# Angles, peaks and tables moved between a pair's maximum and its scale, and one-column sums set between long products

## The chip, the cores and the metric

One core of one Trainium2 chip runs the whole kernel in one launch. The metric is the device time of that core in microseconds (us), median of several runs. The engines are called PE (TensorE, matrix products), DVE (VectorE), ACT (ScalarE), POOL (GpSimd) and SP (SyncE, which here only issues DMAs). PSUM is where PE writes.

## The reference, cut to what matters

```python
# layer 0: x -> x + concat(pool mixer, short conv mixer, each gated by silu) @ w_out_ab
# layer 1, for 1024 tokens, 1024 channels, 16 heads:
h = rms_norm(x, norm_c)
c_q, c_kv, k_rope, z = split(h @ w_in_c, [768, 1024, 1056])
q  = rms_norm(c_q, q_lat_norm) @ w_uq      # needs the mean square of c_q over 768 channels, per token
kv = rms_norm(c_kv, kv_lat_norm) @ w_ukv   # and of c_kv over 256 channels
cos, sin = cos(positions * inv_freq), sin(positions * inv_freq)
q, k = rope_tail(rms_norm(q, q_head_norm), cos, sin), rope_tail(rms_norm(k, k_head_norm), cos, sin)
x = x + (causal_attention(q, k, v) * silu(z)) @ w_out_c
```

Everything is float32. The change lies in the first half of layer 1: the input projection `h @ w_in_c`, the tables of cosine and sine, and the mean squares of `c_q` and `c_kv`.

## The kernel before, in words

Channels lie on the 128 partitions, the 1024 tokens along the free dimension. Each engine has one program, in a fixed order, written out by hand as a function (`sync`, `scalar`, `vector`, `gpsimd`, `tensor`); semaphores join them. An engine does nothing behind a wait until the wait is over. Numbers are split into a high and a low part, and every product is made of three matmuls (`three_passes`, lines 111 to 113): high by high, high by low, low by high.

Layer 1's input projection has two kinds of output tiles. The four plain gate tiles `Z0` to `Z0+3` (the last is `ROPE0-1`) and the tile `ROPE0` of the rotary key are products with float32 parts, 48 matmuls a tile, 32 for `ROPE0`, each 128x512. The other twelve tiles are made two at a time, as pairs 8 to 13 (`PAIRED` is 8, `GATE_PAIRS` is 12, `ALL_PAIRS` is 14): pairs 8 to 11 give the latents `c_q` and `c_kv`, pairs 12 and 13 the last four gate tiles. A pair is made Strassen-like from seven products (`pair_product(p, i)`, i from 0 to 6) of float16 parts; each is 12 matmuls of 128x512, in four chunks `c` of three.

For a pair p+1 to be ready, this chain runs while PE works on pair p:

- DVE takes the largest weight of the raw tiles (`pair_peak`, line 1071, out `w_row`); PE spreads it over partitions with one one-column float32 product against `ones` (`row_sum`, line 1562) after product 2 of pair p, and waits there if the maximum is late;
- DVE turns it into a scale (`pair_scale`, lines 1080 to 1082), after which ACT writes the seven high parts (`pair_forms`, line 720) and DVE the seven low parts (`pair_low`, line 1088);
- between them DVE makes three quarters of pair p's output from PSUM (`quarter`, line 1101) as products 3, 4 and 5 of it end, and ACT makes snapshots of products 0, 1 and 2 (`snapshot`, line 727). Product i of 2, 3, 4 waits for snapshot i-2, and product 6 waits for the second quarter. POOL makes the sums of raw weights that four of the forms need (`left_sums`), and adds squares of the latents (`square_sums`, line 634).

Other work of DVE hangs in this loop at the end of an iteration: `angles(0)` and `angles(1)` (the rotary angles, brought into the range of the sine), `peaks` (the largest weights of `w_ukv`), `tables` (14 table and gain instructions, lines 1145 to 1158, from the sine that ACT makes at line 873), `rope_and_roots` (line 1164 on, which begins with the mean squares of the latents and ends with the semaphore `roped`). The mean squares come from 16 one-column products of PE with the squares as weights (line 1599), all in a row after product 5 of pair 12. In the same way `token_sums` (line 1617) makes 8 in a row inside tile `Z0`.

In the last pair DVE writes the low parts of six latents (`lat_low`, line 1209) and of the first weights of the next stage (line 1318). The next stage's first product waits for `roped`, for all eight `lat_low` and for all eight low parts of those weights. The gates of pair 12 are multiplied by the roots by POOL (line 649), those of pair 13 by DVE (`late_gate`, line 1260).

Of the kernel before, what the change touches and what calls it, by code (L numbers as in the profile page):

```python
# [20 lines left out]
ALU = mybir.AluOpType  # L21
AX_X, AX_XY = mybir.AxisListType.X, mybir.AxisListType.XY

P = 128
# [162 lines left out]
def front(nc, x_t, gamma, w_in, pool_w, pool_scale, conv_w, w_out, x1_t, gamma1, w_lat, positions, q_lat_g, kv_lat_g,  # L187
# [408 lines left out]
    def gpsimd(pool):  # L596
# [47 lines left out]
        for m in range(2):  # L644
            dest_m = pair_dest(GATE_PAIRS, m)
            pool.wait_ge(c_done, 3 * (GATE_PAIRS + 1))
            pool.wait_ge(c21_done, GATE_PAIRS + 1)
            pool.wait_ge(roped, 1)
            nc.gpsimd.tensor_tensor(dest_m, dest_m, rstd_all[:], ALU.mult).then_inc(gate_scaled, 1)

    def scalar(act):
# [210 lines left out]
        def later_paired():  # L862
            for p in range(PAIRED, ALL_PAIRS):
                last_pair = p + 1 == ALL_PAIRS
                late_square = PAIRED + 2 <= p < GATE_PAIRS
                if PAIRED < p <= GATE_PAIRS:
                    latent_squares(p - 1, range(1 if late_square else 2))
                snapshot(p, 0)
                if p == PAIRED:
                    plain_silu(PLAIN_GATES - 1)  # L870
                if p == PAIRED + 1:
                    act.wait_ge(reduced, 2)
                    nc.scalar.activation(trig[:], red[:], ACT.Sin).then_inc(trig_done, 1)
                if p == GATE_PAIRS - 1:
                    latent_high(1)
                if p == GATE_PAIRS:
                    latent_high(3)
                if last_pair:
                    latent_high(0)
                snapshot(p, 1)  # L880
                if p == GATE_PAIRS - 1:
                    latent_high(2)
                if p == GATE_PAIRS:
                    latent_high(4)
                if last_pair:
                    for m in (KQ, KQ + 1):
                        latent_high(m)
                if late_square:
                    latent_squares(p - 1, [1])
                snapshot(p, 2)  # L890
                if last_pair:
                    latent_high(KQ - 1)
                if not last_pair:
                    pair_forms(p + 1, range(FORMS))
                else:
                    first_weights()
                last_quarter(p)
            act.wait_ge(gate_scaled, 2)
            for m in range(2):
                gate_silu(PLAIN_GATES + m)  # L900
            act.wait_ge(last_scaled, 2)
            for m in range(2):
                gate_silu(PLAIN_GATES + 2 + m)
# [39 lines left out]
    def vector(dve):  # L943
# [312 lines left out]
        def late_gate(m):  # L1256
            dest_m = pair_dest(GATE_PAIRS + 1, m)
            dve.wait_ge(c_done, 3 * ALL_PAIRS)
            dve.wait_ge(c21_done, ALL_PAIRS)
            nc.vector.tensor_tensor(dest_m, dest_m, rstd_all[:], ALU.mult).then_inc(last_scaled, 1)  # L1260
# [6 lines left out]
        def later_paired():  # L1267
            for p in range(PAIRED, ALL_PAIRS):
# [3 lines left out]
                if p == PAIRED:  # L1272
                    angles(0)
                if p == GATE_PAIRS - 1:
                    top()
# [4 lines left out]
                else:  # L1280
                    for j in range(2, LAT - 1):
                        lat_low(j)
# [20 lines left out]
                if p == PAIRED:  # L1303
                    angles(1)
                if p == PAIRED + 1:
                    peaks()
                if p == PAIRED + 2:
                    tables()
# [4 lines left out]
            for m in range(2):  # L1313
                late_gate(m)
# [121 lines left out]
        right_sums(0)  # L1436
        roots(2, ms1, rstd1, tmp1, sums[:, 0])
        right_sums(1)
        rights(0)
# [19 lines left out]
    def tensor(pe):  # L1459
# [26 lines left out]
        def tile(n):  # L1486
            pe.wait_ge(lo_done, n - RING + len(STEPS) + 1)
            slot_free(n)
            if n == Z0:
                for k in range(NK):  # L1490
                    pe.wait_ge(x1_done, k + 1)
                    for c in range(2):
                        last = product(n, k, c, k == 0, k == NK - 1)
                    if k == CHUNKS:
# [3 lines left out]
                    if k == NK - 2:  # L1498
                        pe.wait_ge(x1_added, OUT_TILES - 1)
                        token_sums()  # L1500
            else:
                for c in range(2):
                    for k in range(NK):
                        if n == OUT0 - 1 and c == 0 and k == CHUNKS:
                            row_sum(0)
                        if n == ROPE0 - 1 and c == 1 and k == CHUNKS:
# [6 lines left out]
        def first_out_tiles():  # L1513

            for part in (range(NK - 2), range(NK - 2, NK)):
                for n in (OUT0, OUT0 + 1):
# [7 lines left out]
                    if part.stop == NK:  # L1524
                        last.then_inc(proj_ready, 1)

        def pair_product(p, i):
# [17 lines left out]
            for c in range(CHUNKS):  # L1545
                if p == 0 and i in (2, 4, 6):
                    pe.wait_ge(act_low, FIRST_FORMS + (i // 2 - 1) * CHUNKS + c + 1)
                if p == PAIRED:
# [3 lines left out]
                                    right(p, i, 0, c), right(p, i, 1, c), fresh and c == 0, c == CHUNKS - 1, not fresh)  # L1552
            last.then_inc(pair_ready, 1)

# [18 lines left out]
        def later_paired():  # L1573
            for p in range(PAIRED, ALL_PAIRS):
                for i in range(FORMS):
# [17 lines left out]
                    if p == GATE_PAIRS and i == 5:  # L1593
                        pe.wait_ge(topped, 2)
                        pe.wait_ge(lat_summed, LAT - 2)
                        for part in range(2):
                            for t in range(NT):
                                col = part * NT + t
                                last = nc.tensor.matmul(small_ps[:, col:col + 1], sq[:, part, t * P:(t + 1) * P],
                                                        ones[:, 0:1], start=True, stop=True)  # L1600
                        last.then_inc(small_ready, 1)
# [12 lines left out]
        def token_sums():  # L1614

            for t in range(NT):
                last = nc.tensor.matmul(pooled[:, t:t + 1], sums[:, 0, t * P:(t + 1) * P], ones[:, 0:1],
                                        start=True, stop=True)
            last.then_inc(summed, 1)
# [982 lines left out]
```

## Time and profile before

| | |
|---|---|
| median of 3 runs | 995.08 us (995.02 to 995.61) |
| the profiled execution | 995.0 us, span 993.2 us |
| mean granted TensorE clock | 0.988 of 2.4 GHz |
| PE busy | 968.5 us, 98% of the span |
| DVE busy | 796.8 us, 80% |
| ACT busy | 563.2 us, 57% |
| POOL busy | 319.1 us, 32% |

Busy means that the engine had an instruction in work; a share near 100% of one engine says that it bounds the time, though not that each of its instructions ran at full speed. The granted clock says at which speed PE was let run: 1.00 is 2.4 GHz, 0.50 is 1.2 GHz. The span runs from the first to the last instruction; 1.8 us of the execution's time lie around it.

### The profile page before, as it was taken

The numbers are of one execution on the slowest core, as the hardware profiler recorded it, in microseconds if no ns is written. First come the engines' busy times: TensorE is split into PE (matmuls) and PEld (weight loads), VectorE is DVE, ScalarE is ACT, GpSimd is POOL, SyncE is SP. The second block draws the span as 40 slices with busy tenths as digits, with TensorE's granted clock in tenths as the row PEclk, the third lists the DMA queues.
The fourth block names the chain that finished last, engine by engine and source line by source line (L and its number), as shares of the span: only waits on it lengthen the run. The fifth ranks groups of instructions, "written<-read, shape, count | busy, mean of one in ns | idle before, by whom it ended". The sixth has DMA issues, their size and how long they took to land.

```text
span 993.2 us, 16008 instructions
## 1 busy us (share of the span) xinstructions
PE 968.5 (98%) x5858; PEld 709.3 (71%) x5858; DVE 796.8 (80%) x1363; ACT 563.2 (57%) x1049; POOL 319.1 (32%) x381
## 2 busy tenths in 40 slices
PE   9999999999999998989799999999999999999998
PEld 8788444444788887534356999997777888887887
DVE  5798899998765599878687799998999999996311
ACT  7443554335243372535437667867999999997000
POOL 0002342240000002236133477876864335551000
PEclk9999999999999999989889999999999999999999
DMA  9310421111154430413022164567587656430322
GB/s 296 61 50 12 111 80 43 45 41 43 64 170 146 129 86 19 153 44 82 1 69 81 37 213 137 204 196 187 112 212 155 160 127 115 108 108 1 116 85 75
DMA packets 165341, 103.65 MB, mean 104 GB/s; under 512 B 75272, under 2 KB 149520, under 8 KB 165008
## 3 DMA queue, kind: packets, MB, share of 16 engines
q1 hardware_dynamic: 159216, 102.25, 36.7%
q10 hardware_dynamic: 6048, 0.39, 0.5%
q8 instruction: 47, 0.77, 0.3%
q14 instruction: 30, 0.25, 0.1%
HBM read 56.48 MB, written 29.36 MB: 86 GB/s over the span
## 4 chain that ended last, share of the span: by engine, by line
PE 79%; DVE 16%; issue 3%; ACT 2%; DVEq 0%; POOL 0%; ACTq 0%; POOLq 0%
PE banks L111 22%; PE banks L113 22%; PE banks L112 22%; PE banks L2405 6%; PE banks L2423 3%; PE banks L2424 1%; DVE front_w_row L1071 1%; DVE lat_lo L1209 1%; DVE heads_probs_big L2213 1%; DVE front_lt L1229 1%; PE banks L1635 1%; PE banks L2432 1%; ACT heads_probs_big L2086 1%; DVE heads_pt_lo L2221 1%; DVE front_l L1229 1%
## 5 line engine op out<-in xcount | busy, mean ns | idle before, releaser
L2221 DVE TENSOR_TENSOR heads_pt_lo<-banks,heads_pt_hi 128x512 f16<-128x512 f32 (+2 forms) x192 | 102.0, 554 | 11.3 <-ACT heads_pt_hi L2095 6.9
L2095 ACT ACTIVATE heads_pt_hi<-banks 128x512 f16<-128x512 f32 (+2 forms) x192 | 88.4, 485 | 4.9 <-PE banks L2405 4.7
L2423 PE MATMUL banks<-heads_v,heads_pt_hi 128*128 128x128 f16 x576 | 74.6, 220 | 0.0
L2405 PE MATMUL banks<-ident,heads_probs_big 128*128 128x128 f32 x416 | 69.1, 279 | 1.4 <-ACT heads_probs_big L2086 1.3
L2424 PE MATMUL banks<-heads_v,heads_pt_lo 128*128 128x64 f16 x576 | 69.5, 193 | 0.0
L2213 DVE CUSTOM_DVE_ANT_0 heads_probs_big<-banks,heads_mask,score_scale 128x1024 f32<-128x1024 f32 (+1 forms) x64 | 68.5, 1071 | 0.9
L2086 ACT ACTIVATE heads_probs_big<-heads_probs_big,heads_neg_max 128x1024 f32<-128x1024 f32 (+1 forms) x64 | 63.4, 991 | 5.3 <-DVE heads_neg_max L2213 3.3
L111 PE MATMUL banks<-front_act_hi,front_w_hi 128*128 128x512 f32 x160 | 64.4, 403 | 0.0
L111 PE MATMUL banks<-heads_k_t,heads_q_t 96*128 96x512 f16 (+2 forms) x192 | 62.9, 327 | 0.9 <-DVE heads_neg_max L2213 0.9
L112 PE MATMUL banks<-front_act_lo,front_w_hi 128*128 128x512 f32 x160 | 62.9, 393 | 0.0
L113 PE MATMUL banks<-front_act_hi,front_w_lo 128*128 128x512 f32 x160 | 62.8, 393 | 0.0
L112 PE MATMUL banks<-heads_k_t,heads_q_t 96*128 96x512 f16 (+2 forms) x192 | 62.3, 324 | 0.0
L113 PE MATMUL banks<-heads_k_t,heads_q_t 96*128 96x512 f16 (+2 forms) x192 | 61.5, 325 | 0.0
L1747 DVE TENSOR_TENSOR out_res<-banks,out_res 128x512 f32<-128x512 f32 x16 | 10.9, 690 | 59.5 <-PE banks L113 59.5
L2423 PEld LDWEIGHTS banks<-heads_v,heads_pt_hi 128*128 128x128 f16 x576 | 54.1, 99 | 1.1 <-DVE heads_pt_lo L2221 0.3
L2338 POOL TENSOR_TENSOR heads_o_sum<-heads_o_raw 128x256 f32<-128x256 f32 x32 | 23.3, 728 | 94.0 <-ACT heads_o_raw L2102 93.6
L2424 PEld LDWEIGHTS banks<-heads_v,heads_pt_lo 128*128 128x128 f16 x576 | 51.3, 98 | 2.2
L2405 PEld LDWEIGHTS banks<-ident,heads_probs_big 128*128 128x128 f32 x416 | 46.7, 141 | 7.7 <-DVE heads_pt_lo L2221 3.3
L111 PE MATMUL banks<-out_gate_hi,out_w_hi 128*128 128x512 f32 x128 | 50.4, 394 | 0.4 <-DVE w_out_lo L1728 0.2
L111 PE MATMUL banks<-front_y_hi,front_w_hi 128*128 128x512 f32 x128 | 50.0, 391 | 0.0
L113 PE MATMUL banks<-out_gate_hi,w_out_lo 128*128 128x512 f32 x128 | 49.9, 390 | 0.0
L112 PE MATMUL banks<-gate_lo,out_w_hi 128*128 128x512 f32 x128 | 49.8, 389 | 0.0
(435 smaller groups left out, 3027.6 us busy)
## 6 DMA issues: line engine op xcount, KB each, us to landing
qk_scratch<-heads_y SPq DMA_DIRECT2D x22, 512.0 KB, 3.6
front_x<-in_x_t SPq DMA_DIRECT2D x16, 512.0 KB, 5.1
front_raw<-in_w_in_ab SPq DMA_DIRECT2D x14, 512.0 KB, 5.1
qk_scratch<-heads_last_y SPq DMA_DIRECT2D x10, 512.0 KB, 4.1
front_w<-in_w_out_ab SPq DMA_DIRECT2D x8, 512.0 KB, 3.7
x_scratch<-front_x SPq DMA_DIRECT2D x8, 512.0 KB, 4.0
v_scratch<-heads_v SPq DMA_DIRECT2D x32, 128.0 KB, 3.0
heads_v_st<-v_scratch SPq DMA_DIRECT2D x8, 512.0 KB, 5.3
```

The costliest lines, as they stand in the source:

```text
L111: nc.tensor.matmul(out, w_hi, a_hi, start=first, stop=False, skip_group_check=resumed)
L112: nc.tensor.matmul(out, w_hi, a_lo, start=False, stop=False, skip_group_check=resumed)
L113: return nc.tensor.matmul(out, w_lo, a_hi, start=False, stop=last, skip_group_check=resumed)
L1229: nc.vector.scalar_tensor_tensor(right_split(c, part, 1), right_source(c, part), later_scale[:, 0:1], right_split(c, part, 0), ALU.mult, A ...
L2086: nc.scalar.activation(row, row, ACT.Exp, bias=neg_max[:, h % 2, i:i + 1], scale=-1.0, accum_out=total[:, h % 2, i:i + 1]).then_inc(exp_do ...
L2095: nc.scalar.activation(pt_hi[:, q % PIECES, :width], t_ps[:, banks[("piece", n, k)] % 3, :width], ACT.Copy).then_inc(pt_high, 1)
L2213: nc.vector.tensor_tensor_reduce(probs(n, 0, width), scores(i, 0, width), mask[:, S - width:], score_scale[:], 3e38, ALU.add, ALU.min, neg ...
L2221: nc.vector.tensor_tensor(pt_lo[:, q % PIECES, :width], t_ps[:, banks[("piece", n, k)] % 3, :width], pt_hi[:, q % PIECES, :width], ALU.sub ...
L2338: nc.gpsimd.tensor_tensor(o_sum[:, g % 2], raw[:, :, :VH], raw[:, :, VH:], ALU.add).then_inc(o_summed, 1)
L2405: last = nc.tensor.transpose(t_ps[:, b, r * P:(r + 1) * P], probs(n, j * P, (j + 1) * P), ident[:])
L2423: nc.tensor.matmul(out, pt_hi[:, q % PIECES, blk], v2[e][:, j, :], start=(j == 0), stop=False)
L2424: last = nc.tensor.matmul(out[:, :VH], pt_lo[:, q % PIECES, blk], v2[e][:, j, :VH], start=False, stop=(j == i))
```

## The change

Four things change, and no instruction's size:

1. On DVE, `angles(1)`, `peaks` and `tables` leave the end of iterations 8, 9 and 10 and stand in iterations 9, 10 and 11 behind `pair_peak` of the next pair and ahead of its `pair_scale`. `angles(0)` stands there already. ACT's sine (line 873) moves from behind snapshot 0 to behind snapshot 2 of pair 9.
2. PE's `row_sum(8)` moves from the middle of the second half of tile `ROPE0-1` into the middle of the first half of `ROPE0`.
3. The 16 one-column sums of the latents are set two by two behind the first, second and third chunk of products 3, 4 and 5 of pair 12 (eight places), and the 8 of `token_sums` two by two behind the last four groups of tile `Z0`. On DVE `right_sums(1)` and two low parts of `rights(0)` now stand ahead of `roots(2)`, which waits for those sums.
4. The multiplication of pair 12's two gate tiles goes from POOL to DVE, one each behind the first two `lat_low` of the last iteration.

```diff
@@ gpsimd
-        for m in range(2):
-            dest_m = pair_dest(GATE_PAIRS, m)
-            pool.wait_ge(c_done, 3 * (GATE_PAIRS + 1))
-            pool.wait_ge(c21_done, GATE_PAIRS + 1)
-            pool.wait_ge(roped, 1)
-            nc.gpsimd.tensor_tensor(dest_m, dest_m, rstd_all[:], ALU.mult).then_inc(gate_scaled, 1)
@@ scalar, later_paired
                 snapshot(p, 0)
-                if p == PAIRED + 1:
-                    act.wait_ge(reduced, 2)
-                    nc.scalar.activation(trig[:], red[:], ACT.Sin).then_inc(trig_done, 1)
...
                 snapshot(p, 2)
+                if p == PAIRED + 1:
+                    act.wait_ge(reduced, 2)
+                    nc.scalar.activation(trig[:], red[:], ACT.Sin).then_inc(trig_done, 1)
@@ vector, later_paired
                     pair_peak(p + 1)
                 if p == PAIRED:
                     angles(0)
+                if p == PAIRED + 1:
+                    angles(1)
+                if p == PAIRED + 2:
+                    peaks()
                 if p == GATE_PAIRS - 1:
+                    tables()
                     top()
...
                     pair_scale(p + 1)
                 else:
-                    for j in range(2, LAT - 1):
+                    for m in range(2):
+                        lat_low(2 + m)
+                        late_gate(GATE_PAIRS, m)
+                    for j in range(4, LAT - 1):
                         lat_low(j)
...
-                if p == PAIRED:
-                    angles(1)
-                if p == PAIRED + 1:
-                    peaks()
-                if p == PAIRED + 2:
-                    tables()
@@ vector
         right_sums(0)
+        right_sums(1)
+        rights(0, range(2))
         roots(2, ms1, rstd1, tmp1, sums[:, 0])
-        right_sums(1)
-        rights(0)
+        rights(0, range(2, SIX))
@@ tensor, tile
                         last = product(n, k, c, k == 0, k == NK - 1)
+                        if k >= NK - 2:
+                            if k == NK - 2 and c == 0:
+                                pe.wait_ge(x1_added, OUT_TILES - 1)
+                            turn = 2 * (k - NK + 2) + c
+                            token_sums(range(2 * turn, 2 * turn + 2))
...
-                    if k == NK - 2:
-                        pe.wait_ge(x1_added, OUT_TILES - 1)
-                        token_sums()
...
-                        if n == ROPE0 - 1 and c == 1 and k == CHUNKS:
+                        if n == ROPE0 and c == 0 and k == CHUNKS:
                             row_sum(PAIRED)
@@ tensor, pair_product
+                if p == GATE_PAIRS and i in LATENT_TURNS and c < CHUNKS - 1:
+                    for n in range(2):
+                        latent_sum(6 * LATENT_TURNS.index(i) + 2 * c + n)
...
+        def latent_sum(col):
+            if col == 0:
+                pe.wait_ge(topped, 2)
+                pe.wait_ge(lat_summed, LAT - 2)
+            if col < 2 * NT:
+                part, t = divmod(col, NT)
+                one = nc.tensor.matmul(small_ps[:, col:col + 1], sq[:, part, t * P:(t + 1) * P],
+                                       ones[:, 0:1], start=True, stop=True)
+                if col == 2 * NT - 1:
+                    one.then_inc(small_ready, 1)
```

`LATENT_TURNS` is (3, 4, 5). The 16 sums in a row of the old place (after product 5 of pair 12) are taken out.

## Rows read from the trace of the kernel before

**Rows 1.** The page's first section, busy time of each engine.

```profile
PE 968.5 (98%) x5858; PEld 709.3 (71%) x5858; DVE 796.8 (80%) x1363; ACT 563.2 (57%) x1049; POOL 319.1 (32%) x381
```

**Rows 2.** PE's waits, 340 to 540 us: total us, times, longest.

```profile
PE banks L1562 <- DVE front_w_row L1071: 9.9, 3, 6.6
PE banks L1562 <- DVE front_held L1254: 3.2, 1, 3.2
PE banks L111 <- DVE joint_uq_lo L1318: 1.6, 1, 1.6
```

**Rows 3.** Busy time by stretch, then granted clock (third from the end), DMA share, GB/s.

```profile
389.60:392.80 3.20, 3.20 (x10) 2.52 (x10) 3.20 (x5) 0.00 (x0) 0.00 (x0) 0.50 0.00 0
430.80:437.40 6.60, 6.10 (x16) 2.52 (x17) 2.01 (x6) 4.40 (x7) 0.00 (x0) 0.50 0.00 0
475.00:481.80 6.80, 3.51 (x10) 1.58 (x11) 4.73 (x9) 2.24 (x4) 0.44 (x1) 0.50 0.01 2
509.00:516.00 7.00, 7.00 (x24) 3.92 (x24) 5.62 (x20) 0.00 (x0) 0.00 (x0) 0.51 0.60 186
```

**Rows 4.** Timeline of PE: start, duration, instruction, idle before it and releaser.

```profile
351.17 1.84 PE L1617 MATMUL banks<-front_ones,front_sums 128*128 128x1 f32 x16
...
389.37 0.36 PE L1562 MATMUL banks<-front_w_row,front_ones 128*128 128x1 f32 x2 [3.18 <-DVE front_held L1254]
...
401.29 0.39 PE L111 MATMUL banks<-front_l,front_set_even 128*128 128x512 f16 x1
...
431.30 0.59 PE L1562 MATMUL banks<-front_w_row,front_ones 128*128 128x1 f32 x2 [3.05 <-DVE front_w_row L1071]
...
478.29 0.59 PE L1562 MATMUL banks<-front_w_row,front_ones 128*128 128x1 f32 x2 [6.61 <-DVE front_w_row L1071]
...
498.75 0.28 PE L1562 MATMUL banks<-front_w_row,front_ones 128*128 128x1 f32 x2
498.89 0.38 PE L111 MATMUL banks<-front_l,front_set_even 128*128 128x512 f16 x1
...
506.66 4.65 PE L1599 MATMUL banks<-front_ones,front_sq 128*128 128x1 f32 x32
511.17 0.59 PE L111 MATMUL banks<-front_lt,front_set_even 128*128 128x512 f16 x1
...
535.99 0.47 PE L111 MATMUL banks<-joint_kv_hi,joint_lat_hi 128*128 128x512 f32 x1 [1.63 <-DVE joint_uq_lo L1318]
```

**Rows 5.** Timeline of DVE, the blocks that move and what stands behind them.

```profile
395.70 1.22 DVE L1254 TENSOR_TENSOR front_held<-banks,front_rstd_all 128x1024 f32<-128x1024 f32 x1
...
445.13 4.41 DVE L1183 TENSOR_REDUCE front_w_peak<-front_wide 128x8 f32<-128x4096 f32 x1
...
464.01 0.34 DVE L1145 TENSOR_REDUCE front_peak<-front_head_g 128x2 f32<-128x192 f32 x1
...
475.95 2.29 DVE L1071 TENSOR_REDUCE front_w_row<-front_raw_even 128x1 f32<-128x2048 f32 x1
...
480.31 0.75 DVE L1088 SCALAR_TENSOR_TENSOR front_set_even<-front_raw_even,front_w_scale,front_set_even 128x512 f16<-128x512 f32 x1 [0.85 <-ACT front_set_even L720]
...
511.34 0.37 DVE L1164 SCALAR_TENSOR_TENSOR front_ms<-banks,front_eps 128x8 f32<-128x8 f32 x2 [0.83 <-PE banks L1599]
...
518.39 10.27 DVE L1209 SCALAR_TENSOR_TENSOR lat_lo<-latent,front_gam_lat,joint_lat_hi 128x1024 fp32r<-128x1024 f32 x5
528.58 1.40 DVE L1101 SCALAR_TENSOR_TENSOR gate<-banks,front_unscale,front_later_snap 128x512 f32<-128x512 f32 x2
...
535.77 2.35 DVE L1260 TENSOR_TENSOR gate<-gate,front_rstd_all 128x1024 f32<-128x1024 f32 x2
```

**Rows 6.** Timeline of ACT around the start of pair 8.

```profile
402.41 2.94 ACT L827 ACTIVATE gate<-front_held 128x1024 f32<-128x1024 f32 x3
405.25 0.67 ACT L727 ACTIVATE front_later_snap<-banks,front_unscale 128x512 f32<-128x512 f32 x1
```

**Rows 7.** Timeline of POOL, the gates of pair 12.

```profile
518.64 6.54 POOL L649 TENSOR_TENSOR gate<-gate,front_rstd_all 128x1024 f32<-128x1024 f32 x2 [17.02 <-DVE rms_v L1178]
```

More of the change, by code:

```diff
@@ L1254, in plain_gate, with late_gate @@
             nc.vector.tensor_tensor(held[i][:], proj[:, ring_bank(Z0 + i)], rstd_all[:], ALU.mult).then_inc(evacuated, 1)
[L1256 to L1260, printed above, removed]
+        def late_gate(p, m):
+            dest_m = pair_dest(p, m)
+            dve.wait_ge(c_done, 3 * (p + 1))
+            dve.wait_ge(c21_done, p + 1)
+            nc.vector.tensor_tensor(dest_m, dest_m, rstd_all[:], ALU.mult).then_inc(
+                gate_scaled if p == GATE_PAIRS else last_scaled, 1)
         def first_weights(j, name, k):
@@ L1313, in later_paired @@
             for m in range(2):
-                late_gate(m)
+                late_gate(GATE_PAIRS + 1, m)
         def w_low(j, lo, raw, hi):
@@ L1525, in first_out_tiles @@
                         last.then_inc(proj_ready, 1)
+        LATENT_TURNS = (3, 4, 5)
         def pair_product(p, i):
@@ L1592, in later_paired @@
                                          top_diag[0:VGROUPS, :], start=True, stop=True).then_inc(top_spread, 1)
[L1593 to L1601, printed above, removed]
         def pool_map(g):
@@ L1612, in pool_map, with token_sums @@
             last.then_inc(pool_ready, 1)
-        def token_sums():
-            for t in range(NT):
+        def token_sums(part=range(NT)):
+            for t in part:
                 last = nc.tensor.matmul(pooled[:, t:t + 1], sums[:, 0, t * P:(t + 1) * P], ones[:, 0:1],
                                         start=True, stop=True)
-            last.then_inc(summed, 1)
+            if NT - 1 in part:
+                last.then_inc(summed, 1)
         def spread_roots(n, diagonal):
```

## The prediction

> **What bounds the kernel now.** The page comes first: PE is busy for 98% of the span, no other engine for more than 80% [rows 1]. So only what makes PE wait, or run slowly, or do more, counts. The list of PE's waits in the stretch of the change shows five, 14.7 us together: three for a pair's maximum (3.05, 0.2 and 6.6 us), one of 3.2 for a gate tile, one of 1.6 before the next stage's first product [rows 2]. The stretches by granted clock show what these cost besides: four stretches at 0.50, which is the 1.2 GHz level, 23.6 us in all, against 1.00 in the rest of the run [rows 3]. The timeline of PE ties them together: the clock fell 2.7 to 3.6 us after PE had become idle at 386.0, 428.1 and 471.5, and 2.3 us after the 16 one-column sums began, and came back 3.2 to 7.0 us later [rows 3, 4]. The wait of 1.63 us at 534 had no such stretch behind it.
>
> **The unit.** 36 matmuls of 128x512 at the high level take from 498.89 to 506.66, 0.216 each, so a product of 12 takes 2.59 us; a row sum between them costs 498.89 - 498.75 = 0.14 [rows 4]. The float32 ones take 0.227. At the low level the same work takes twice as long, so a us of it loses half a us.
>
> **Tile Z0.** The 8 token sums are 16 passes of PE in 1.70 us, 0.106 each [rows 4]. Two by two, each place has four passes, the first with its weight load behind a long matmul as in a row sum: 0.14 + 2 x 0.106 = 0.35, four places 1.4. Gain 0.3. DVE's `roots(2)` begins about 4 us later but ends near 360.6, and PE wants it at 360.9: hidden by 0.3 us, what it costs if that is gone is the excess. DVE no longer waits for the sums, so its chain runs 0.3 us ahead to 400 us.
>
> **Row sum 8.** PE idled 3.18 us for it and then lost 1.6 to the clock (3.2 us at half) [rows 3, 4]. In its new place it comes 12 + 8 matmuls later, 4.5 us, near 390.3, when the maximum and the gate tile (389.2) are there. From 385.75, half a tile, `ROPE0` and the sum take 2.72 + 7.25 + 0.14, so PE reaches pair 8 at 395.9 instead of 401.29. But there it meets what it never met: gate tile `ROPE0-1`, written by DVE at 395.70 + 1.22 [rows 5], 0.3 earlier now, so it starts at 396.65 (a wait of 0.8). Product 2 wants snapshot 0 at 401.8; ACT first makes its high forms (to 398.4), the copy of the rotary tile and three silus of 2.94 together [rows 6], so the snapshot ends near 402.8: a wait of 1.0. Net, 3.6 us ahead from here.
>
> **Pair 9 (angles).** The block of 8.2 us stood before the maximum; now PE's wait of 3.05 and the 3.1 lost to the clock (14 matmuls and a sum in 6.2 instead of 3.15) go: 6.3 us [rows 2 to 4]. The block ends about 9.0 us into the pair, 0.9 behind the row sum; forms and low parts follow, and the second quarter is made 14.0 us in, product 6 wants it at 15.7: hidden by 1.7. The sine and its wait move behind snapshot 2, where ACT's queue holds only the forms, which wait for the scale anyway: nothing.
>
> **Pair 10 (peaks).** The wait of 0.2 goes, with what is lost around it 0.5 [rows 2]. The 5.5 us block (4.41 us its reduction [rows 5]) ends 8.2 us into the pair, when the row sum is just there: nothing on the path.
>
> **Pair 11 (tables).** 464.01 to 475.95 is the block, then the maximum [rows 5]. The wait of 6.61 goes, and 1.8 of clock: 8.5 us [rows 2 to 4]. But now the scale waits for the block. The maximum takes 2.2, beside two of POOL's additions; then each table instruction that meets a POOL addition waits it out (they took 1.2 to 2.3 us instead of 0.3), so the block ends 12.4 us into the pair. Scale, forms, low parts and quarters: the second quarter is done 3.5 us after the scale begins (1.4 to the first low part, 478.91 to 480.31 [rows 5], then four steps of 0.66 less overlap), near 16.4; product 6 wants it at 16.05. A new wait of 0.35. Bounds: 0, if POOL's additions fall under the maximum, and 2.6 with no saving from them. I take 0.35. Net 8.2.
>
> So pair 12 begins 3.6 + 6.3 + 0.5 + 8.2 = 18.6 us earlier: at 472.4 instead of 491.0.
>
> **Pair 12 and 13 to the next stage.** Before, this was 535.99 - 490.99 = 45.0 us. The sums took 4.51 us and the clock lost 2.3 behind them [rows 4]; in eight places of 0.35 they take 2.8, and the clock should hold. PE gains 4 us, but PE doesn't set the end here: DVE does. Its chain: low parts and quarters follow products 4 and 5, which now hold sums and end 2.1 and 2.8 us later in the pair. Product 5 ends 18.5 us in, the third quarter and three low parts take 0.66 each behind it, so `rope_and_roots` begins 21.3 us in (20.35 before: 511.34 [rows 5]), and needs 7.05 to 518.39. Then six `lat_low`, at 1.19 each alone; five took 10.2 beside POOL's gates, two of them 3.38 each while POOL multiplied for 6.54 [rows 5, 7]. With POOL gone five take 5.95, but the two gates cost DVE 2 x 1.17 [rows 5]: 8.3 instead of 10.2. The rest is unchanged, 7.4 us from 528.58 to 535.99. 21.3 + 7.05 + 8.3 + 7.4 = 44.0: a gain of 1.0 only. PE now waits 1.5 for the second quarter of pair 13 (DVE 21.3 + 7.05 + 8.3 + 1.4 = 38.1; PE 13 products of 2.59, the row sum and 2.8 for the sums, 36.6) and 3.3 before the next stage (PE 38.1 + 2.6 = 40.7, DVE 44.0).
>
> **The clock again.** Both idle stretches of 3.2 us fell to the low level; 1.6 us did not. Ours is 3.3, with 1.5 shortly ahead. I take it that it falls, and loses what the rows lost after an idle stretch, 1.6 to 3.1, say 2.2. In the Trainium skill (TensorE: Matmul & The Clock Gate, HAM oscillation) waits between bursts of matmuls drop the clock each time; the rows of this trace agree, and that page alone would also put the fall here.
>
> **Sum.** 18.6 + 1.0 - 2.2 = 17.4 against the execution's own 995.0 (span 993.2 and 1.8 around it; the median is the same within 0.1): 977.6. I say 977.5. Behind 536 us PE is busy 98% and the engines shift together, so nothing is given back there.
>
> **Rivals.**
>
> - *The clock holds through the new wait before the next stage.* For it: in one idle stretch the fall came only with PE's restart (3.6 us). Against: all three such stretches fell. 975.4. Chance 0.25.
> - *The forecast*, 976 to 979.5: 0.50.
> - *The blocks between maximum and scale take the wait's place:* DVE stays behind by more than 0.35 at a second quarter, the one of the tables above all. Price: up to 2.6 in pair 11, some more where pairs 8 and 9 start close to DVE, and a fall of the clock behind it, 1.7 to 3. 980 to 984. For it: DVE has under 2 us of slack in pair 9 and none in 11. Chance 0.15.
> - *Short products inside the long ones bring the clock down.* Against: the row sum in each pair, a short product between long ones, never did. For: the 16 in a row did. If pair 12's products 3 to 6 run at the low level, about 11 us lose 5.5 to 8: 983 to 986. In the Trainium skill (the same page, A second HAM failure mode) small idles between groups make the clock oscillate; no row here shows it. Chance 0.05.
> - *Slower than before:* the same mechanism without a return. From the first split sums, through both new waits, into the next stage PE stays at 1.2 GHz. It decides from 20 us lost, so 40 us at the low level; at 50 us the time is 1000. The longest such stretch in the trace is 7.0 [rows 3]. Chance 0.02.
> - *The change does nothing:* the waits have another cause than the order. Against: the releaser of the two large ones is the maximum, with DVE busy right up to it [rows 4, 5]. 995. Chance 0.03 with everything near it.
>
> **Numbers.** 973.5 to 982.5 holds the first two and most of the third: a little over 8 in 10. The likeliest one's own range is 976 to 979.5. A measurement of this kernel tells 0.2%, 2 us, from no change. Faster 0.96, same 0.02, slower 0.02.
>
> **What would show it.** In the profile after: no wait of PE at lines 1562 in pairs 8, 9 and 11 and no stretch at 0.50 before pair 13; waits of about 0.8 for the held gate and 1.0 for a snapshot at pair 8's start; the second quarter of pair 11 within 0.5 us of product 6; five `lat_lo` no longer 3.38 us; 16 sums in eight groups with the clock at 1.00; one wait of some 3.3 us before the first product of `joint_kv_hi`, now near 516, and a short stretch at 0.50 behind it. The prediction is wrong if a block delays a pair by more than a us, if the split sums drop the clock, or if DVE's chain in pairs 12 and 13 is not the 44.0 us worked out.

## The result and the profile after

The changed kernel takes 977.98 us (median of 4 runs, 976.37 to 978.10); the kernel before took 995.05 beside it (4 runs, 994.61 to 995.61). The ratio is 0.9824, with a 95% interval of 0.9807 to 0.9841: 17.1 us less. The profiled execution has a span of 976.3 us against 993.2. The page's first section after, to hold against [rows 1]:

```profile
PE 959.5 (98%) x5858; PEld 705.9 (72%) x5858; DVE 789.5 (81%) x1365; ACT 563.0 (58%) x1049; POOL 312.5 (32%) x379
```

PE is still the only engine above 81%. Its busy time fell by 9.0 us with the same 5858 instructions: by the stretches below that is mostly work that no longer runs at 1.2 GHz. The rest is idle time. The list of PE's waits after, 340 to 540 us, answers to [rows 2] (total, times, longest):

```profile
PE banks L111 <- DVE joint_uq_lo L1315: 3.1, 1, 3.1
PE banks L111 <- DVE gate L1095: 1.4, 1, 1.4
PE banks L111 <- DVE latent L1095: 1.0, 1, 1.0
PE banks L111 <- issue: 0.6, 1, 0.6
PE banks L111 <- DVE front_held L1248: 0.4, 1, 0.4
```

No wait for a pair's maximum is left; five waits, 6.5 us together, stand where 14.7 stood. Four are at new places; the fifth is the old one before the next stage's first product, grown from 1.6 to 3.1. The stretches by granted clock (columns as in [rows 3]):

```profile
518.10:521.40 3.30, 3.30 (x11) 3.11 (x10) 1.74 (x3) 2.15 (x3) 1.99 (x3) 0.50 0.82 303
360.00:520.00 160.00, 153.48 (x725) 86.10 (x724) 142.97 (x206) 81.37 (x114) 49.87 (x34) 0.99 0.26 76
```

The four old slow stretches are gone. One of 3.3 us has come at another place; it begins 1.0 us behind the end of the largest wait. The timeline of PE after, at its waits and row sums (columns as in [rows 4]):

```profile
350.30 0.50 PE L1625 MATMUL banks<-front_ones,front_sums 128*128 128x1 f32 x4
351.46 0.50 PE L1625 MATMUL banks<-front_ones,front_sums 128*128 128x1 f32 x4
...
390.42 0.28 PE L1579 MATMUL banks<-front_w_row,front_ones 128*128 128x1 f32 x2
396.67 0.38 PE L111 MATMUL banks<-front_l,front_set_even 128*128 128x512 f16 x1 [0.37 <-DVE front_held L1248]
402.59 0.38 PE L111 MATMUL banks<-front_lt,front_set_even 128*128 128x512 f16 x1 [0.58 <-issue]
424.19 0.28 PE L1579 MATMUL banks<-front_w_row,front_ones 128*128 128x1 f32 x2
460.83 0.28 PE L1579 MATMUL banks<-front_w_row,front_ones 128*128 128x1 f32 x2
470.36 0.38 PE L111 MATMUL banks<-front_lt,front_set_odd 128*128 128x512 f16 x1 [1.03 <-DVE latent L1095]
480.71 0.28 PE L1579 MATMUL banks<-front_w_row,front_ones 128*128 128x1 f32 x2
511.21 0.38 PE L111 MATMUL banks<-front_lt,front_set_odd 128*128 128x512 f16 x1 [1.42 <-DVE gate L1095]
517.08 0.47 PE L111 MATMUL banks<-joint_kv_hi,joint_lat_hi 128*128 128x512 f32 x1 [3.12 <-DVE joint_uq_lo L1315]
```

The row sums are marks along the way, since PE does the same work between them in both kernels except for what is moved. R8 to R13 are the row sums of pairs 8 to 13, H is the next stage's first product; times in us from the span's start, out of the timelines of PE:

| | R8 | R9 | R10 | R11 | R12 | R13 | H | H to the end |
|---|---|---|---|---|---|---|---|---|
| before | 389.37 | 409.07 | 431.30 | 453.03 | 478.29 | 498.75 | 535.99 | 457.2 |
| after | 390.42 | 405.17 | 424.19 | 442.46 | 460.83 | 480.71 | 517.08 | 459.2 |

H comes 18.9 us earlier; 2.0 of it is given back behind H, where the slow stretch lies. 16.9 is the difference of the spans. A second mark stands ahead of everything that changed: the one-column product for `x_row`, at 348.21 before and 348.03 after.

### The profile page after: what moved, and what is told of

It is laid out like the page before. It is cut to its first block, busy times and chain, and to the rows that moved or that the text cites. A ratio compares the mean times of both kernels' runs of the same rounds, so it can differ in the third digit from the quotient of the medians.

```text
span 976.3 us, 16009 instructions
## 1 busy us (share of the span) xinstructions
PE 959.5 (98%) x5858; PEld 705.9 (72%) x5858; DVE 789.5 (81%) x1365; ACT 563.0 (58%) x1049; POOL 312.5 (32%) x379
## 4 chain that ended last, share of the span: by engine, by line
PE 68%; DVE 23%; issue 3%; POOL 3%; ACT 3%; DVEq 0%; POOLq 0%; ACTq 0%
PE banks L111 19%; PE banks L113 18%; PE banks L112 18%; PE banks L2414 6%; PE banks L2432 3%; PE banks L2433 2%; DVE heads_y L2213 1%; DVE heads_x L2208 1%; POOL heads_prod L2319 1%; DVE heads_x L2209 1%; DVE front_lt L1223 1%; DVE heads_ss L2255 1%; DVE heads_probs_big L2222 1%; DVE front_l L1223 1%; DVE front_w_row L1065 1%
## 6 DMA issues: line engine op xcount, KB each, us to landing
qk_scratch<-heads_y SPq DMA_DIRECT2D x22, 512.0 KB, 3.8
front_x<-in_x_t SPq DMA_DIRECT2D x16, 512.0 KB, 5.2
front_raw<-in_w_in_ab SPq DMA_DIRECT2D x14, 512.0 KB, 5.1
qk_scratch<-heads_last_y SPq DMA_DIRECT2D x10, 512.0 KB, 3.9
front_w<-in_w_out_ab SPq DMA_DIRECT2D x8, 512.0 KB, 3.7
x_scratch<-front_x SPq DMA_DIRECT2D x8, 512.0 KB, 3.9
heads_v_st<-v_scratch SPq DMA_DIRECT2D x8, 512.0 KB, 5.5
```

## Experiments

Each is compared with runs of the kernel before on its own chip. R13 to H is read from each profile; profiled executions differ by up to 1.7 us in when they reach the product for `x_row`, so such intervals compare better than spans.

| kernel | median us (range, runs) | before, us | ratio, 95% | R13 to H |
|---|---|---|---|---|
| blocks alone | 980.55 (978.88 to 980.85, 5) | 994.95 | 0.9847, 0.9834 to 0.9861 | 36.32 |
| row sum 8 alone | 990.24 (988.66 to 991.89, 5) | 994.95 | 0.9950, 0.9937 to 0.9963 | 37.23 |
| split latent sums alone | 997.18 (995.92 to 998.95, 7) | 994.95 | 1.0025, 1.0014 to 1.0036 | 38.29 |
| change, latent sums in a row | 976.03 (974.47 to 977.23, 4) | 994.95 | 0.9808, 0.9794 to 0.9821 | 34.38 |
| change, gates on POOL | 978.47 (977.92 to 980.63, 5) | 994.89 | 0.9843, 0.9828 to 0.9859 | 38.28 |
| change, gates last | 975.48 (973.78 to 975.79, 4) | 994.89 | 0.9805, 0.9791 to 0.9820 | 34.07 |
| change, key early | 972.98 (972.82 to 973.07, 4) | 994.89 | 0.9783, 0.9770 to 0.9797 | 33.28 |
| key early, sums in a row | 976.11 (973.73 to 977.32, 4) | 994.89 | 0.9812, 0.9794 to 0.9830 | 37.23 |
| key early, gates last | 973.86 (973.33 to 974.57, 4) | 994.83 | 0.9794, 0.9781 to 0.9807 | 33.29 |
| ... and low parts first | 972.42 (971.47 to 972.63, 4) | 994.83 | 0.9777, 0.9764 to 0.9791 | 31.37 |
| ... and gains split off | 970.39 (970.22 to 971.36, 5) | 994.83 | 0.9763, 0.9749 to 0.9776 | 31.36 |
| change, token sums in a row | 977.84 (977.13 to 979.17, 4) | 994.83 | 0.9835, 0.9822 to 0.9849 | 36.35 |

**Blocks alone.** The kernel before with part 1 of the change.

```diff
                 if p == PAIRED:
                     angles(0)
+                if p == PAIRED + 1:
+                    angles(1)
+                if p == PAIRED + 2:
+                    peaks()
                 if p == GATE_PAIRS - 1:
+                    tables()
                     top()
...
```

> The kernel before with part 1 of the change alone: angles, peaks and tables between maximum and scale, the sine behind snapshot 2. Theory (the blocks account for nearly all): pair 9 loses its wait and slow stretch (6.3 us), pair 10 0.5, pair 11 8.5 less the new wait of 1.0 for the second quarter; the next stage's first product moves 14.3 us ahead and keeps its wait of 1.6, so no slow stretch behind it: 980.8 us. Rival (the blocks only take the wait's place, and the row sum and the sums gave the gain): 985 us or more.

Measured 14.4 us less than before: the blocks are most of the change. From the product for `x_row` at 348 us to R8 nothing moved (41.16 in both), and R9 to R11 takes 37.29 (409.93 to 447.22), the same as in the changed kernel. The timeline of PE has this for its 16 latent sums, against 4.65 in [rows 4]:

```profile
493.38 3.63 PE L1598 MATMUL banks<-front_ones,front_sq 128*128 128x1 f32 x32
```

and the granted clock is 1.00 in it. Behind the row it fell after all, from 497.2 to 500.7, so the mean of this stretch is 0.65:

```profile
496.00:500.00 4.00, 4.00 (x18) 2.07 (x19) 3.59 (x15) 0.00 (x0) 0.00 (x0) 0.65 0.34 105
```

That cost nothing, since PE waited for DVE later anyway (R13 to H is 1.94 longer than with the sums in a row below, where the clock held, and the gates account for 1.91). The wait before the next stage was 2.4 where 1.6 had been expected, and behind it the clock stayed at 1.00 (H to the end: 457.2). The move of the sine was not tried by itself.

**Row sum 8 alone.** The kernel before with one condition of PE changed.

```diff
-                        if n == ROPE0 - 1 and c == 1 and k == CHUNKS:
+                        if n == ROPE0 and c == 0 and k == CHUNKS:
                             row_sum(PAIRED)
```

> The kernel before with part 2 alone, row sum 8 half a tile and a half later. Theory: PE loses the wait of 3.2 us and 1.6 of slow clock, pays 0.4 for the gate tile and 0.6 for the snapshot at pair 8, and reaches pair 9 3.9 us earlier; DVE's blocks follow PE, so the later waits stay as they were and the 3.9 us come through: 991.2 us. Rival (DVE sets the pace in pair 9, so PE only waits longer for the maximum there): 995 us.

From the product for `x_row` to R9 it takes 57.49 instead of 60.86: 3.4 less, with two new waits at pair 8 in it, 0.76 for the gate tile and 0.58 for snapshot 0 (see the section on the prediction). The median is 4.7 less. The profiled run is the slowest of the five, with a mean clock of 0.990 where the others have 0.991 to 0.994; the rest of the gain is theirs, and no trace shows where their clock stayed up.

**Split latent sums alone.** The kernel before with the latent half of part 3: two sums behind each of the first three chunks of products 3, 4 and 5 of pair 12.

```diff
+                if p == GATE_PAIRS and i in LATENT_TURNS and c < CHUNKS - 1:
+                    for n in range(2):
+                        latent_sum(6 * LATENT_TURNS.index(i) + 2 * c + n)
...
-                    if p == GATE_PAIRS and i == 5:
...
```

> The kernel before with the 16 latent sums two by two, nothing else. Theory (DVE's chain sets the end of pair 13): products 4 and 5 of pair 12 end later, so roots and low parts end 0.9 us later; PE saves 4 us there but waits 3.3 us for the second quarter of pair 13 and 3.5 before the next stage, and the clock falls, 1.7 to 3.4 more: slower than before, 998 us. Rival (what PE saves comes through): 4 us of passes and clock, up to 6.8, less: 988 to 991 us.

Slower than before, by 0.25%, and the interval excludes 1. The timeline of PE shows a new wait for the second quarter, as expected (3.3), and that the wait before the next stage stayed as it was, where 3.5 had been expected:

```profile
532.34 0.58 PE L111 MATMUL banks<-front_lt,front_set_odd 128*128 128x512 f16 x1 [3.35 <-DVE gate L1101]
538.20 0.47 PE L111 MATMUL banks<-joint_kv_hi,joint_lat_hi 128*128 128x512 f32 x1 [1.62 <-DVE joint_uq_lo L1318]
```

R13 to H is 1.05 longer than before. The clock fell at 532.0, and product 6, which starts at 532.34, took 4.1 us instead of 2.6: that is why the last wait is short, and it cost nothing, since DVE sets the time of H. The rest of the difference is not the split's, whose sums come later: three intervals ahead of R13 differ from the kernel before, R8 to R9 by 1.35 more, R10 to R11 by 1.27 less, R12 to R13 by 1.28 more (21.74 instead of 20.46), each by how long the clock stayed low behind an old wait. Behind the one of 6.6 us it came back near 484 instead of 481.6. So slow stretches behind equal waits differ by over a us from one execution to the next. What the other runs had was not seen.

**The change with its latent sums in a row.** The old place and form, the rest as changed.

```diff
-                if p == GATE_PAIRS and i in LATENT_TURNS and c < CHUNKS - 1:
...
+                    if p == GATE_PAIRS and i == 5:
...
```

> The changed kernel with the 16 latent sums again in a row behind product 5 of pair 12. Theory (DVE's chain sets the end): DVE starts the roots 1 us earlier and ends 43.1 us into pair 12, PE with its sums and slow clock ends at 43.3; no wait and no slow stretch before the next stage: 975.5 us, faster than the changed kernel by 2.4. Rival (split sums are a gain): 981 to 985 us.

```profile
488.60 3.63 PE L1613 MATMUL banks<-front_ones,front_sq 128*128 128x1 f32 x32
515.08 0.47 PE L111 MATMUL banks<-joint_kv_hi,joint_lat_hi 128*128 128x512 f32 x1 [2.10 <-DVE joint_uq_lo L1315]
```

(timeline of PE.) R13 to H is 34.38 instead of 36.37: the split costs 1.99 us here. The clock is 1.00 in the row, behind it, and behind the wait of 2.10. The medians say the same, 1.95, but their intervals overlap. Where it comes from stands on DVE: `rope_and_roots` begins 11.67 behind R13 with the row (11.68 in the blocks-alone kernel) and 13.65 with the split. With the row it is this line of DVE's timeline:

```profile
492.37 0.35 DVE L1158 SCALAR_TENSOR_TENSOR front_ms<-banks,front_eps 128x8 f32<-128x8 f32 x2
```

In a row the sums run while DVE makes the third quarter and three low parts; split, they stand ahead of product 5's end, for which that quarter waits. Eight places of 0.35 and the 2.7 us from the quarter's start to the roots' begin, less the 3.63 of the row, make 1.9.

**The change with pair 12's gates on POOL.** Part 4 undone; POOL's loop, not shown here, comes back.

```diff
-                    for m in range(2):
-                        lat_low(2 + m)
-                        late_gate(GATE_PAIRS, m)
-                    for j in range(4, LAT - 1):
+                    for j in range(2, LAT - 1):
                         lat_low(j)
```

> The changed kernel with pair 12's two gate multiplications back on POOL, behind the semaphore roped. Theory (DVE and POOL shut each other out): two low parts take 3.4 us instead of 1.2, which is 2 us more than the two multiplications cost DVE itself, and all of it is on DVE's chain: the next stage starts 1.9 us later, 980 us, up to 981.5 if the slow stretch grows. Rival (a gate is off the path on either engine): 975.6 us, as DVE has 2.35 us less to do.

R13 to H is 1.91 longer, as forecast from 10.2 against 8.3 for five low parts and two gates. The timelines of DVE and POOL:

```profile
501.33 10.28 DVE L1209 SCALAR_TENSOR_TENSOR lat_lo<-latent,front_gam_lat,joint_lat_hi 128x1024 fp32r<-128x1024 f32 x5
...
501.59 6.55 POOL L649 TENSOR_TENSOR gate<-gate,front_rstd_all 128x1024 f32<-128x1024 f32 x2 [18.08 <-DVE rms_v L1178]
```

Yet the median is only 0.5 longer. PE now waits 3.34 for the second quarter of pair 13, and the clock falls in that wait: the slow stretch, 512.0 to 518.8, comes before H, where PE would have waited for DVE anyway, and nothing is lost behind it (H to the end: 457.2). The first part of the stretch by clock:

```profile
512.00:515.00 3.00, 1.92 (x5) 0.72 (x6) 3.00 (x5) 0.00 (x0) 0.00 (x0) 0.50 0.00 0
```

**Gates last.** Pair 12's two gates go behind the last low part of the first weights, ahead of pair 13's.

```diff
-                    for m in range(2):
-                        lat_low(2 + m)
-                        late_gate(GATE_PAIRS, m)
-                    for j in range(4, LAT - 1):
+                    for j in range(2, LAT - 1):
                         lat_low(j)
...
+            for m in range(2):
+                late_gate(GATE_PAIRS, m)
+            for m in range(2):
                 late_gate(GATE_PAIRS + 1, m)
```

> The changed kernel with pair 12's two gate multiplications on DVE, but behind the last low part of the weights. Theory (DVE's chain, shorter by 2.35 us): the wait for the second quarter of pair 13 goes, the wait before the next stage is 2.5 us; 975.6 us with the slow stretch, 974.0 without. Rival (the silus, now 2.4 us later, hold ACT and so the first evacuations of the next stage): no gain, 978 us.

R13 to H is 2.30 shorter. The wait is 2.40, and in this execution the clock fell at 514.5, 0.2 us before its end:

```profile
514.69 0.76 PE L111 MATMUL banks<-joint_kv_hi,joint_lat_hi 128*128 128x512 f32 x1 [2.40 <-DVE joint_uq_lo L1314]
```

```profile
514.60:517.60 3.00, 2.91 (x7) 2.36 (x8) 3.00 (x3) 0.75 (x1) 2.85 (x4) 0.50 0.96 322
```

(timeline of PE, and the stretch by clock.) H to the end is 458.7, so 1.5 went back.

**Key early.** The part of `rope_and_roots` that needs no sums (the rotary key) goes into pair 12 between maximum and scale, where DVE waits for the row sum of pair 13. `roped` is then given as soon as the roots are done.

```diff
                 if p == GATE_PAIRS:
                     v_scales()
+                    rope_key()
```

> The changed kernel with the rotary key's part of rope_and_roots (12 of its instructions, 4.5 us, which need neither the sums nor the latents) moved into the 4.4 us in which DVE waits for row sum 13. Theory: DVE's chain is 4.5 us shorter and PE with its split sums sets the end of pair 13, 39.2 us into pair 12 with a wait of about 0.4: 971.9 us, no slow stretch. Rival (POOL's additions of squares lie in that gap and the moved instructions wait them out, so that the scale of pair 13 is late): 975 us or more.

R13 to H is 3.09 shorter, the clock 1.00 throughout. The wait for the second quarter of pair 13 is gone. One of 1.62 is left before the next stage, where 0.4 had been expected:

```profile
513.88 0.47 PE L111 MATMUL banks<-joint_kv_hi,joint_lat_hi 128*128 128x512 f32 x1 [1.62 <-DVE joint_uq_lo L1320]
```

**Key early, sums in a row.** Both edits together.

> e7 with the 16 sums in a row again. Theory (the split is worth something only where PE is the bound): PE with the row and its slow clock ends 43.3 us into pair 12, DVE long before: 975.5 us, the same as the changed kernel with the row alone, and 3.6 to 4 us slower than e7. Rival (the row's place matters as little as in the changed kernel): 972 us.

R13 to H is 3.95 longer than with the split. Now PE sets the time in pairs 12 and 13, and the row costs PE both its length and a low clock behind it:

```profile
488.55 4.33 PE L1618 MATMUL banks<-front_ones,front_sq 128*128 128x1 f32 x32
```

```profile
491.50:498.50 7.00, 7.00 (x22) 3.35 (x23) 6.59 (x20) 0.44 (x1) 0.00 (x0) 0.53 0.29 88
```

(timeline of PE, and the stretch by clock.) The median is 3.1 longer than with the split. How much of that is the clock, the runs suggest: one of the four had a mean clock of 1.000 and took 973.73, 0.75 above the median with the split, while the other three, at 0.996 to 0.998, took 975.12 to 977.32. By that the row's own length costs under a us, and the fall of the clock in and behind it the rest; no trace of the one run was kept.

**Key early, gates last.** Two reasons were left for the 1.62: DVE's queue as a whole, which shorter work ahead would pull in, or the work behind the second quarter alone, which can't start before product 4 of the last pair has ended.

> e7 and e6 together: key part early, pair 12's gates behind the last low part of the weights. In e7 PE still waits 1.62 us before the next stage, the same as in the kernel before and in e2 and e8. Theory (a floor: behind the second quarter of pair 13, which follows product 4, DVE has a fixed run of 6.5 us, and PE only 2 products): DVE has 2.35 us less ahead of it, but the wait stays 1.6: 972.9 us, as e7. Rival (DVE's whole chain is still the bound): 971.3 us.

R13 to H stays at 33.29, and the wait at 1.62: the second.

**... and low parts first.** In the last pair `lat_low(7)` and the two low parts of `w_ukv` move ahead of the second quarter.

```diff
-                quarter(p, 1)
                 if last_pair:
                     lat_low(LAT - 1)
                     for k in range(KKV):
                         first_weights(k, "kv", k)
+                quarter(p, 1)
```

> e9 with the last latent's low part and the low parts of the two kv weights ahead of the second quarter of pair 13. Theory (the fixed run is the floor, so shorten it by 2.4 us): no wait before the next stage, 1.6 us less than e7 and e9: 971.3 us. Rival (the second quarter then comes late and product 6 waits instead): 972.9 us or more.

No wait is left before H; R13 to H falls by 1.92 to 31.37 (more than the 1.62 of the wait, because the next stage's first matmul now starts only 0.07 behind the one ahead of it and overlaps its end). So the work behind the second quarter was the floor.

**... and gains split off.** The first six instructions of `tables`, which need no sine, move into pair 9 behind `pair_scale`.

```diff
                     pair_scale(p + 1)
+                    if p == PAIRED + 1:
+                        gains()
```

> e10 with the first six instructions of tables (gains, no sine needed) moved from pair 11 to pair 9, behind the scale. Theory (DVE is 1 us late at the second quarter of pair 11 for the block): the block is 0.9 to 3.4 us shorter, the wait of 1.0 goes: 970.3 us. Rival (POOL's additions fill the block whatever stands in it): no gain, 971.3 us.

The wait of 1.03 in pair 11 is gone, and R12 to R13, in which it lies, takes 18.68 instead of 19.88. The scale begins 22.31 us behind R11 instead of 23.61: the six instructions had taken 3.7 us of the block, but the eight that stay and one of `top` (1.87 instead of 0.15) meet more of what POOL adds. The list of PE's waits, 340 to 545 us, has two lines left:

```profile
PE banks L111 <- issue: 0.6, 1, 0.6
PE banks L111 <- DVE front_held L1255: 0.4, 1, 0.4
```

This is the fastest of all: 970.39, 24.4 us below the kernel before.

**Token sums in a row.** The 8 one-column sums of tile `Z0` and DVE's order there as before.

> The changed kernel with the 8 token sums of tile Z0 in a row and DVE's roots, right sums and low parts in the old order. Theory, after the trace of the changed kernel (four places of 0.47 us between float32 products against 1.80 in a row): PE gains nothing by the split; DVE waits 0.3 for the sums, and of that at most 0.4 shows as a wait at pair 8: 978.0 to 978.4 us. What the prediction said: 0.3 us more on PE and 0.3 on DVE's chain, 978.3 to 978.6.

By time it can't be told from the change. In the changed kernel's timeline above, a place of four passes and three matmuls of 0.227 take from 350.30 to 351.46, so a place costs 0.48 and four 1.9. In a row the sixteen passes hold back the next matmul by 1.70 and the one behind it by 0.09 more, 1.8: no gain. What the reordering on DVE gives is seen at the gate tile: the wait is 0.75 in this kernel and 0.37 in the changed one, and R8 to R9 takes 15.14 against 14.75.

## Why the prediction was right

977.5 was forecast, 977.98 measured, inside the likeliest case's own range of 976 to 979.5, and the profile shows its mechanism in all stages but for one size. Two of its own signs came out against it, both in pair 11: the second quarter was to be within 0.5 us of product 6 and was 0.87 late, and a block that delays a pair by more than a us was to prove it wrong, which 1.03 just does. By its steps:

- **Tile Z0:** gain forecast 0.3, measured none; the price of a place was 0.48 and not 0.35. The 0.3 that DVE was to run ahead became 0.4 at the gate tile, as the token experiment shows.
- **Row sum 8:** the waits forecast at 0.8 and 1.0 were 0.37 and 0.58, both at the places named. The profile names no releaser for the second ("issue"), but ACT's timeline has snapshot 0 ending at 402.49, and product 2 starts 0.1 later; in the kernel with the row sum alone it is 403.16 and again 0.1.

```profile
401.82 0.67 ACT L721 ACTIVATE front_later_snap<-banks,front_unscale 128x512 f32<-128x512 f32 x1
```

  From the product for `x_row` at 348 us to R9 it was 60.86 before and is 57.14: 3.7, where 3.6 was forecast net.
- **Pairs 9 and 10:** R9 to R11 went from 43.96 to 37.29, 6.7 us; forecast 6.3 + 0.5 = 6.8. (The prediction's wait of 3.05 and clock loss of 3.1 make 6.15, not 6.3.)
- **Pair 11** is where a size was off. R11 to R13 went from 45.72 to 38.25, 7.5 us; forecast 8.2. The term that was mis-sized is the new wait of 0.35: it was 1.03. The timeline of DVE has it all:

```profile
462.35 3.30 DVE L1152 SCALAR_TENSOR_TENSOR front_ktab<-front_trig,front_head_g 128x128 f32<-128x128 f32 x4
465.68 0.28 DVE L1189 TENSOR_REDUCE front_tops<-banks 4x1 f32<-4x128 f32 x1
465.99 0.15 DVE L1190 TENSOR_TENSOR front_top_diag<-ident,front_tops 4x4 f32<-4x4 f32 x1
466.07 0.16 DVE L1074 TENSOR_SCALAR front_w_size<-banks 128x1 f32<-128x1 f32 x1
...
467.47 0.75 DVE L1082 SCALAR_TENSOR_TENSOR front_set_even<-front_raw_even,front_w_scale,front_set_even 128x512 f16<-128x512 f32 x1 [0.85 <-ACT front_set_even L714]
...
469.46 0.74 DVE L1095 SCALAR_TENSOR_TENSOR latent<-banks,front_unscale,front_later_snap 128x512 f32<-128x512 f32 x1
```

  Product 6 started at 470.36 behind 1.03 of idle, so it was wanted at 469.33, and by the forecast's 16.05 the pair began at 453.28. The block then ended 12.4 us into the pair (465.65), as forecast. `top`, which was not in the sum by name, put 0.4 behind it. From the scale to the end of the second quarter it took 4.13 (466.07 to 470.20) where 3.5 was forecast: 1.40 to the first low part as in [rows 5], then four steps of 0.67 and no overlap. The forecast's own terms, 12.4 and 3.5, make 15.9; its 16.4 has 0.5 that it does not name, enough for `top`. What it had wrong is the overlap of the four steps, which it took off without a row for it. That makes 16.9 instead of 16.4, and PE started 0.16 later still. The experiment that takes six instructions out of the block removed the wait, so it is shown that the block is on its path. That is the rival of the blocks that take the wait's place, at 0.7 us instead of up to 2.6.
- **Sum to R13:** 17.9 earlier, counted from 348 us; forecast 18.6. The miss is that of pair 11.
- **Pairs 12 and 13:** forecast 45.0 to 44.0. R13 to H fell by 0.87. DVE's chain on its timeline:

```profile
494.36 0.36 DVE L1158 SCALAR_TENSOR_TENSOR front_ms<-banks,front_eps 128x8 f32<-128x8 f32 x2
...
501.41 1.28 DVE L1203 SCALAR_TENSOR_TENSOR lat_lo<-latent,front_gam_lat,joint_lat_hi 128x1024 fp32r<-128x1024 f32 x1
502.61 1.22 DVE L1254 TENSOR_TENSOR gate<-gate,front_rstd_all 128x1024 f32<-128x1024 f32 x1
...
506.07 3.67 DVE L1203 SCALAR_TENSOR_TENSOR lat_lo<-latent,front_gam_lat,joint_lat_hi 128x1024 fp32r<-128x1024 f32 x3
509.66 1.40 DVE L1095 SCALAR_TENSOR_TENSOR gate<-banks,front_unscale,front_later_snap 128x512 f32<-128x512 f32 x2
```

  Pair 12 begins at 472.94, so the roots begin 21.4 us in (forecast 21.3). From 494.36 to 501.41 the roots take 7.05, from there to 509.66 five low parts and two gates take 8.25, and 7.42 follow to H: the terms were 7.05, 8.3 and 7.4. PE's waits were forecast at 1.5 and 3.3 and are 1.42 and 3.12.
- **The clock:** forecast a fall behind the last wait, price 2.2; it fell, price 2.0. The delays that the prediction read (2.7 to 3.6 us from the start of an idle stretch to the fall) are 2.3 to 3.4 in stretches of 0.1 us; here the fall came 4.1 us after PE had become idle, 1.0 after it had started again. One of the four runs, 976.37, had a mean granted clock of 1.000 where the other three had 0.998: so the rival of the clock that holds, with a time of 975.4, very likely came true in it; there is no trace of that run. Nothing in the runs says which of the two comes; the prediction had 0.25 for it.
- **Short products inside long ones** did not bring the clock down: it was 1.00 from 481 to 496, with all sixteen in it.

What the prediction did not draw from its own numbers is that the split of the latent sums is a loss. Its chain of DVE has both terms, roots 0.95 later for the split and low parts 1.9 shorter for the gates, and it gave only their sum, a gain of 1.0. The experiments price them apart. R13 to H with the sums in a row and the gates on POOL is 36.32 where the clock stayed at 1.00 in the row (blocks alone) and 37.24 where it fell in the row (before). On 36.32 the split adds 1.96 (38.28 with the gates on POOL), and the gates on DVE take 1.91 to 1.94 off again: 36.32 + 1.96 - 1.91 = 36.37, which is the changed kernel. So the split was a loss, 1.05 on the kernel before, as the 0.95 says, and 1.99 within the change, where the row it replaced would have been 3.63 and not 4.65 us long. It pays, by 3.95 in that interval, once DVE's chain has been shortened so that PE sets the time and the clock falls in the row.

The Trainium skill (GPSIMD Engine Reference, Key points) says that GpSimd shares its SBUF interfaces with VectorE and contends with those of its instructions that have two SBUF inputs; the runs agree, with 10.28 us for five low parts beside POOL's gates and 6.06 for the same five without (gates last).

## What to carry to other kernels

A block of work that an engine does for later goes where that engine would wait anyway, here between handing out a maximum and getting it back spread; its length against that slack, contention included, decides, and one split of it took away the last 1 us. Splitting short work between long products helps the engine that does it and delays the engine that waits for the long ones: ask which of the two ends last. A fall of the clock cost nothing in three kernels here where PE had to wait for DVE afterwards (blocks alone behind the row, gates on POOL, split sums alone), and 1.5 to 2.0 us where it came at H.

## What the runs showed of the hardware

- Every wait of 2.40 us or more in these traces saw the clock fall in it or within 1.2 us behind it, and none of 2.36 or less did (2.36 in blocks alone, 2.10 with the sums in a row, 1.62 in several). That is no limit: 0.04 us lies between, and the changed kernel's wait of 3.12 has three runs with a mean clock of 0.998 and one with 1.000. Nor is the moment fixed: with the same two waits of 1.4 and 3.1 us, the clock fell 1.0 us after H in the changed kernel and 0.4 us ahead of it with the token sums in a row. What decides stays open.
- The same 32 passes in a row took 3.63 us twice, and 4.33, 4.62 and 4.65 once each, by where in them the clock fell; at 3.63 it was 1.00 throughout, and then fell 0.2 us behind the row in one kernel and not at all in the other.
- A place of four one-column passes costs 0.48 us between float32 products and 0.35 between float16 ones (in the changed kernel two places with three matmuls of 0.216 between them start 1.00 to 1.01 apart), though a pass in a row costs 0.106 to 0.113; what the difference consists of was not tried.
- `TENSOR_REDUCE` was not slowed beside POOL (a maximum took 2.28 at 453.33, while POOL made two additions, and 2.28 at 474.09 with POOL idle for all but the last 0.3); two-input instructions of DVE were: four of 128x128 took 5.79 us at the worst (gains split off), and take 1.27 alone.
